# Recurrent layers' block inverse: a level's two products issued one behind the other, the other work in one group after them

## The reference, cut to what matters

```python
def step(state, inp):
    r_t, w_t, k_t, v_t, kk_t, b_t = inp
    sa = jnp.einsum('bhvk,bhk->bhv', state, kk_t)
    state = (state * w_t[:, :, None, :] - sa[..., None] * b_t[:, :, None, :]
             + v_t[..., None] * k_t[:, :, None, :])
    y = jnp.einsum('bhvk,bhk->bhv', state, r_t)
    return state, y
```

## Time and profile before

| | |
|---|---|
| median of 3 runs | 976.15 us (975.79 to 976.30) |
| the profiled execution | 976.48 us |
| its span | 974.7 us |
| PE busy | 963.9 us, 99% |
| DVE busy | 734.9 us, 75% |
| ACT busy | 529.9 us, 54% |
| granted clock of PE | 0.998 of full speed |
| inverse of l = 1, y of level 1 to y of level 5 | 372.72 to 400.73 us |
| inverse of l = 2, the same | 700.10 to 728.11 us |

### The profile page before, as it was taken

The page is one execution under the profiler, slowest core; times in us unless marked ns, Lnnn a source line. Parts: engine busy times, 40 slices in busy tenths (PEclk is TensorE's granted clock), DMA queues, the critical chain, the costliest instruction groups (busy, mean ns, idle before and its releaser), DMA issues.

```text
span 974.7 us, 17484 instructions
## 1 busy us (share of the span) xinstructions
PE 963.9 (99%) x7270; PEld 865.5 (89%) x7270; DVE 734.9 (75%) x1253; ACT 529.9 (54%) x806; POOL 6.8 (1%) x13
## 2 busy tenths in 40 slices
PE   9999999999999999999999999999999999999997
PEld 8999898888888989889988888898887998888886
DVE  6978688877785998867787875568978578787653
ACT  6486566556454653656556553365546466555431
POOL 1000000000000000000000000000000000000000
PEclk9999999999999999999999999999999999999999
DMA  9744445555554332224555455443231255545531
GB/s 339 205 156 170 160 162 198 194 177 206 179 182 158 118 111 88 88 87 144 204 196 205 176 190 200 173 168 115 77 116 54 94 209 187 202 173 197 192 130 44
DMA packets 24823, 156.55 MB, mean 161 GB/s; under 512 B 2736, under 2 KB 4536, under 8 KB 7208
## 3 DMA queue, kind: packets, MB, share of 16 engines
q1 hardware_dynamic: 22320, 151.64, 44.3%
q10 hardware_dynamic: 2072, 2.49, 1.2%
q0 software_dynamic: 352, 1.31, 0.4%
HBM read 153.99 MB, written 1.44 MB: 159 GB/s over the span
## 4 chain that ended last, share of the span: by engine, by line
PE 93%; DVE 3%; issue 1%; ACT 1%; DMA 1%; SPq 0%; DVEq 0%; ACTq 0%
PE bank L507 27%; PE bank L720 22%; PE bank L725 11%; PE bank L751 11%; PE bank L753 6%; PE bank L578 2%; PE bank L1004 1%; PE bank L1022 1%; DVE w_lo L1817 1%; DVE arena L1799 1%; PE bank L583 1%; PE bank L1011 1%; PE bank L965 1%; PE bank L1225 1%; DMA raw<-in_w 1%
## 5 line engine op out<-in xcount | busy, mean ns | idle before, releaser
L1817 DVE TENSOR_TENSOR w_lo<-raw,w_hi 128x2048 fp32r<-128x2048 f32 (+2 forms) x142 | 319.0, 2249 | 111.7 <-ACT w_hi L1288 111.3
L1288 ACT ACTIVATE w_hi<-raw 128x2048 fp32r<-128x2048 f32 (+4 forms) x153 | 273.3, 1788 | 98.6 <-PE bank L753 68.7
L720 PE MATMUL bank<-h_both,w_hi 128*128 128x512 f32 x912 | 228.4, 392 | 0.1
L720 PEld LDWEIGHTS bank<-h_both,w_hi 128*128 128x128 f32 x912 | 164.0, 189 | 29.6 <-issue 0.3
L507 PE MATMUL bank<-h_both,w_hi 128*128 128x256 f32 x880 | 164.0, 287 | 0.2 <-DVE w_lo L1817 0.2
L1288 ACT ACTIVATE arena<-bank 128x256 f32<-128x256 f32 (+3 forms) x189 | 74.0, 403 | 163.6 <-PE bank L725 118.5
L751 PE MATMUL bank<-act_both,w_hi 128*128 128x512 f32 x462 | 162.3, 393 | 0.0
L507 PEld LDWEIGHTS bank<-h_both,w_hi 128*128 128x128 f32 x880 | 137.2, 191 | 5.2 <-issue 2.1
L725 PEld LDWEIGHTS bank<-h_both,w_lo 128*128 128x128 f32 x912 | 124.4, 190 | 8.9
L753 PE MATMUL bank<-act_both,w_lo 128*128 128x256 f32 x462 | 130.6, 283 | 0.0
L725 PE MATMUL bank<-h_both,w_lo 128*128 128x256 f32 x912 | 127.2, 282 | 0.0
(11 more groups left out here) (332 smaller groups left out, 1234.8 us busy)
## 6 DMA issues: line engine op xcount, KB each, us to landing
raw<-in_w SPq DMA_DIRECT2D x136, 1024.0 KB, 4.9
raw<-in_w SPq DMA_DIRECT2D x2, 896.0 KB, 4.5
raw<-in_w SPq DMA_DIRECT2D x3, 512.0 KB, 3.7
raw<-in_w SPq DMA_DIRECT2D x2, 768.0 KB, 4.3
cst<-in_consts SPq DMA_DIRECT2D x1, 1120.0 KB, 11.1
raw<-in_first SPq DMA_DIRECT2D x4, 256.0 KB, 4.7
x<-in_first SPq DMA_DIRECT2D x4, 256.0 KB, 4.9
arena<-bias_rows ACTq DMA_DIRECT2D x4, 256.0 KB, 5.8
```

Of the source, the lines that this page charges most:

```text
L720: pe.matmul(to, hi(k), h_both[:, :, k, :], start=(k == 0), stop=False, skip_group_check=True)
L1288: return act.activation(dst, src, ACT.Copy, **kw)
L1817: dve.tensor_tensor(w_lo[:, s, 0:n], raw[:, s, 0:n], w_hi[:, s, 0:n].bitcast(F32), ALU.subtract)\
```

## The change

On PE, `back_products(n)` follows the y of its level directly for n = 1 to 4, and both halves of `beside_inverse(l, n, ...)` (at n = 1 the whole of `project(l, 8)`) follow behind it. At n = 5 the scores stay between y and `back_products(5)`. y waits for `inv_xt` of the level below; the mark `inv_x` and DVE's wait for it are gone. On DVE the four subtractions of a level move ahead of the level's work beside it, for n = 1 to 4. Two weight splits move too: ACT's `hi_of` of (l, "out", 0) stands ahead of the copies of `up(0)` and `up(1)` instead of behind them; `hi_of` of (l, "out", 1) leaves level 3 for a place behind `exponential(l, 3)`, and DVE's `lo_of` of it goes from ahead of `logits_of(4, 5)` to behind `bonus_and_gain()`.

```diff
-        AFTER_LEVEL = {2: ("out", 0)}
...
                     for q in range(2):
 
                         pe.wait_ge(V.sem, V.at(l, "inv_bt", n, q))
-                        pe.wait_ge(A.sem, A.at(l, "inv0", q)) if n == 1 else pe.wait_ge(V.sem, V.at(l, "inv_x", n - 1, q))
+                        pe.wait_ge(A.sem, A.at(l, "inv0", q)) if n == 1 else pe.wait_ge(V.sem, V.at(l, "inv_xt", n - 1, q))
...
+                    if n == 5:
+                        beside_inverse(l, n, 0)
+                    back_products(n)
                     if n == 1:
-                        project(l, 8, between=lambda: back_products(1))
-                        continue
-                    beside_inverse(l, n, 0)
-                    back_products(n)
-                    if n == 5:
-
-                        break
-                    beside_inverse(l, n, 1)
+                        project(l, 8)
+                    elif n < 5:
+                        beside_inverse(l, n, 0)
+                        beside_inverse(l, n, 1)
...
                             copy(swap_q[:, 0, :], flat(b["qr"])).then_inc(A.sem, A.mark(l, "swap", 2))
-                            hi_of(CHUNK[l, "out", 1])
...
                     for q in range(2):
                         inverse_y(n, q)
+                    if n == 2:
+                        hi_of(CHUNK[l, "out", 0])
                     beside_inverse(n)
-                    if n in AFTER_LEVEL:
-                        hi_of(CHUNK[l, *AFTER_LEVEL[n]])
...
                 exponential(l, 3)
+                hi_of(CHUNK[l, "out", 1])
                 turned(l, 2)
...
-                    beside_inverse(n, 0)
+                    if n == 5:
+                        beside_inverse(n, 0)
                     for q in range(2):
...
-                        after_m(l, "inv_zt", n, q)
+                        else:
+                            after_m(l, "inv_zt", n, q)
                         tt(*(blocks(v, n, 1) for v in (q4(XT, q), q4(XT, q), quads(2 + q)[:, :, 0:64])),
                            ALU.subtract, l, "inv_xt", n, q)
-                        if n == 5:
-                            continue
-                        dve.wait_ge(V.sem, V.at(l, "inv_xt", n, q))
-                        dve.nop().then_inc(V.sem, V.mark(l, "inv_x", n, q))
+                    if n < 5:
+                        beside_inverse(n, 0)
                     beside_inverse(n, 1)
...
                 probs_of(2, 3)
-                lo_of(CHUNK[l, "out", 1])
                 logits_of(4, 5)
...
                 bonus_and_gain()
+                lo_of(CHUNK[l, "out", 1])
```

## The result

| | before | after |
|---|---|---|
| median | 976.54 us (15 runs, 975.79 to 977.21) | 978.28 us (15 runs, 977.95 to 978.68) |
| span of the profiled execution | 974.7 us | 976.6 us |
| PE busy | 963.9 us | 963.5 us |
| y of level 1 to y of level 5, l = 1 | 28.01 us | 27.68 us |
| y of level 1 to `take_off(0)` | 34.94 us | 35.41 us |

The ratio is 1.0019, with an interval of 1.0012 to 1.0026: the changed kernel is slower by 1.74 us. That is just inside the 0.2% that the prediction took as the least that can be told from no change; the interval is narrower than that and excludes no change. All 15 runs of before have a median of 976.54, rather than the 976.15 of the first three.

What follows compares the result with a forecast made beforehand. PE, busy 99% of the span, bounds the kernel. Per layer the inverse gains 0.2 inside a first term of 0.5 to 0.6; the second adds 0.4 to 0.5; 0.95 taken, 1.9 in all, giving 978.1 us, range 975.4 to 980.2.

Steps and rivals of the forecast that it cites:

- the 0.2%: Whole kernel: the least difference, 1.95 us, that a measurement was taken to tell from no change; slower began at 978.1.
- The wait for the copy: PE behind y, levels 1 to 4: pauses 0.22 each for ACT's copy, 0.22 more at level 2; 1.10 per layer.
- The inverse: PE, levels 1 to 4: 1.28 per layer removed less 1.10 of new waiting, a gain of 0.2 us per layer.
- The sum of trips: PE, levels 1 to 4: one small-tile trip spared per level, 0.31 each, 0.22 at level 3; 1.15 per layer.
- The split of (l, "out", 0): DVE behind level 4's subtractions: rotate(3) 0.75 late, take_off(0) 0.6 later, the inverse's gain included; +0.6 per layer.
- The slack: Chain from rotate(3) to take_off(0): 0.11 between the end of negated(0, 0) and take_off(0), with 0.05 for the semaphore.
- The split of (l, "out", 1): DVE behind bonus_and_gain(): idle 0.38 and 0.70, negated(1, 0) 1.08 later, take_off(1) +0.5 per layer; nothing on ACT.
- The sum: Whole kernel: terms of 0.5 to 0.6 and 0.4 to 0.5, taken as 0.95 per layer, 1.9 us slower in all.
- the larger wait: Rival, levels 1 to 4: copy late or PE slower, 0.1 to 0.3 more per level; 980 to 981 us; chance 0.13.
- the first rival: Chain to take_off(0): DVE's delays do not reach PE, only the inverse's 2 x 0.2 gain counts; 975.8 us; chance 0.2.
- DVE's delays do not reach PE: Rival: the chain to take_off(0) has more room than read, only the inverse counts; 975.8 us; chance 0.2.
- the spared trips alone decide: Rival, inverse: copies not waited for, DVE's splits hidden, 2.6 us saved; 973.6 us; chance 0.07.

Runs made afterwards that it cites:

- e6: The changed kernel with 4 idle 64x64 matmuls added between y and the back products at levels 1 to 4: 978.31 us, ratio 1.0018 to the kernel before.
- e7: The changed kernel with 8 idle 64x64 matmuls added between y and the back products at levels 1 to 4: 979.63 us, ratio 1.0032 to the kernel before.
- e10: Changed kernel, both DVE splits moved, level 2's y copied before cq_hi's rounding, first-half copies of y in two 128-column pieces: 974.72 us, 0.9980 to before.
- e3: The changed kernel with both weight splits moved to other places, PE's new order kept: 975.93 us against 976.53 for before, ratio 0.9993.
- e9: The kernel before with only ACT's hi_of of (l, "out", 0) put ahead of the copies of up(0) and up(1): 976.59 us against 976.67, ratio 1.0000.
- e1: The changed kernel with DVE's lo_of of (l, "out", 0) moved from behind level 4's subtractions to ahead of level 3's: 976.74 us, ratio 1.0004 to before.
- e2: Changed kernel, (l, "out", 1) split on DVE back ahead of logits_of(4, 5), on ACT behind level 5's copies of y: 977.61 us, 1.0011 to before.
- e5: The changed kernel with ACT's hi_of of (l, "out", 0) back behind the copies of up(0) and up(1): 985.93 us, ratio 1.0097 to the kernel before.
- e4: The changed kernel with both weight splits moved and PE's order of the kernel before put back: 978.54 us, ratio 1.0022 to the kernel before.

## Why the prediction was right

**The wait for the copy** was priced at 1.16 from y to the back products, 1.38 at level 2, 1.10 a layer. Measured are 1.16 three times and 1.37, and e6, e7 and e10 show the pause from three sides: work put into it costs nothing up to its size, everything beyond it, and a shorter copy gives it back.

**The inverse** gained 0.33 a layer where 0.2 were forecast. Levels 1 and 4 gained 0.12 each, for 0.09 forecast; the terms that were mis-sized are those of levels 2 and 3. At level 2 the forecast was a loss of 0.13 (0.31 for a trip against 0.44 for the wait), and the level gained 0.06. The first two full-array products of `up(0)` stand there. Before, on PE:

```profile
384.07 0.51 PE L507 MATMUL bank<-h_both,w_hi 128*128 128x256 f32 x2
384.42 0.28 PE L507 MATMUL bank<-h_both,w_lo 128*128 128x256 f32 x1
```

and what they read, on DVE, before:

```profile
382.99 1.03 DVE L1799 TENSOR_TENSOR h_both<-spare,h_both 128x512 fp32r<-128x512 f32 x2
```

After, on PE:

```profile
386.34 0.39 PE L504 MATMUL bank<-h_both,w_hi 128*128 128x256 f32 x2
386.57 0.28 PE L504 MATMUL bank<-h_both,w_lo 128*128 128x256 f32 x1
```

0.35 for two products before and 0.23 after, although they follow other full-array products in both. Before, DVE was through with `h_both` at 384.02, and PE began 0.05 later: PE waited here for DVE, in a pause too short for the waits view, and after the change it comes later and doesn't. The product ahead of them also holds PE 0.05 longer before (0.51 against 0.46). Together that is 0.17 of the 0.19 by which level 2 was mis-sized. The sum of trips had no term for that. (That the slow pair comes from the wait is read from these rows; no run tried it.)

At level 3 it was the other way round: 0.13 were forecast as gain (0.22 for the trip, 0.13 for the pause that goes, less 0.22 for the wait), and 0.03 came. The trip was too dear. The new order puts `up(2)` directly in front of `k_rot`, which uses 64x128 tiles:

```profile
393.86 0.28 PE L504 MATMUL bank<-h_both,w_lo 128*128 128x256 f32 x1
394.07 0.70 PE L1181 MATMUL bank<-arena,cst 64*128 64x256 f32 x2
```

0.21 between them, where neighbours of the full array start 0.12 apart: 0.09, the price of getting into smaller tiles once more. In the old order `k_rot` followed the back products, so this change of tile is new, and the trip saves 0.13 rather than 0.22. The other 0.01 is rounding. The mechanism stands, and e3 and e9 size it: of e3's 0.34 the rounding's place is 0.13 and the order of the rest 0.21. That the forecast for the whole inverse missed by no more than 0.13 owes something to luck: one missing term gave 0.19 more, the other took 0.09.

**The split of (l, "out", 0)** was to make `rotate(3)` 0.75 late and `take_off(0)` 0.6. Measured from y of level 1, `rotate(3)` is 0.59 late (29.04 against 28.45) and `take_off(0)` 0.47. The slack was right: 0.12 are lost between the two delays where 0.11 had been read. Too large was the delay at the start, by 0.16: the three levels ahead had won 0.21 instead of 0.15, and the split follows the second half's subtractions 0.40 after their start (399.30 to 399.70), not 0.5. From the end of `negated(0, 0)` to `take_off(0)` it is 0.06, where 0.05 had been taken. The 0.8 of new waiting is 0.79 by e1, but the prediction put all of it at `take_off(0)`: it named ACT's copy of the right side as a link to `negated` and did not see that PE itself waits for that copy at `step(0, 0)`, where 0.26 of it falls. The sum is not changed by that, for `take_off(0)` waits longer for the end of the same chain. e1 shows that both waits go with the split.

**The split of (l, "out", 1)** was to hold `negated(1, 0)` back by 1.08 and `take_off(1)` by 0.45. Measured from `take_off(0)`, they are 0.97 (15.59 against 14.62) and 0.39 later. The two idle stretches in front were priced at 0.38 and 0.70 and are 0.29 and 0.63. e2 shows that this wait goes with this split. On ACT the split costs nothing, as priced: it starts at 411.98, is through in 1.90, and ACT is idle for another 0.56 before `turned(2)`, at 414.44, waiting for PE.

**The sum** was 1.9 us for both layers, and it is 1.72 by the trace and 1.74 by the medians. The first term was given as 0.5 to 0.6 and is 0.47, the second as 0.4 to 0.5 and is 0.39. That the absolute forecast lies so near (978.1 against 978.28) is in part luck: the difference was 0.16 too large, and the median of before, on which it stands, was 0.39 higher than in the first three runs.

**The chances.** Half of the forecast and the larger wait make 0.30 + 0.13 = 0.43 for slower, not 0.45, and the other half and the first rival 0.50, not 0.48. The bound of 0.2% was too wide as well: 0.18% came out clear of no change.

**The rivals.** That DVE's delays do not reach PE falls with the four waits of `take_off`. That the spared trips alone decide falls with the 1.16, although e10 shows how near it was: with the splits in a good place and the copy cut to 1.06, three quarters of the 2.6 us that it promised are there. The larger wait was not in this kernel (1.16 at three levels, 1.37 at level 2), but one instruction's place would have made it: in e5 it costs several times what that rival gave it, by another way, since the copy of y stands there behind a weight split.

## What to carry to other kernels

When products that need one another are put next to each other on PE, the round trip through the copying engine becomes visible (here 1.16 us against 0.94 of work): have nothing ahead of that copy, and copy the first piece separately. Then look for the work on the other engines that the new order pushes back: here two weight splits of 2.2 us that nobody needed soon, in front of a chain without slack, cost more than the new order gave. Such filler is to be moved together with the order, and a new order on one engine alone can be worse than the old order on both or the new one on both (e4 against e9 and e3).

## What was not expected of the hardware

**Behind a pause of 1.68 us PE's clock was halved.** In e5 the granted clock fell after PE had stood still for 1.68 us in the middle of dense work, and stayed at the half level for 8 us and parts of the two stretches beside it, while PE was busy. It fell in both layers of the trace, and all four runs of e5 have a lower mean clock (0.992 or 0.996) than any run of the other kernels (0.998 or 0.999). The pauses of 0.22 to 0.59 us in the inverses of the other kernels moved nothing, nor did two of 0.80 and 0.84 elsewhere in the changed kernel (at 122 and 312 us), behind which the clock is 1.00. The Trainium skill ("TensorE: Matmul & The Clock Gate", section "HAM oscillation — how this bites in real kernels") warns of idle gaps that are longer than this one; by that this pause would have cost its own length alone, and the trace doesn't agree. A section behind it in the Trainium skill, "A second HAM failure mode: psum-queue depth-cycling", tells of very short idle times between groups of matmuls that bring the clock down when they come often; e5 has one long pause a layer, so it doesn't describe this case either.

**DVE and POOL on one SBUF operand pair.** In the changed kernel a DVE operation of 256 columns with both operands in SBUF took 1.05 us while POOL was at work. DVE's row, then POOL's:

```profile
396.09 1.05 DVE L1795 TENSOR_TENSOR spare<-spare 128x256 f32<-128x256 f32 x1
```

```profile
395.58 1.28 POOL L487 TENSOR_TENSOR swap_q<-spare,swap_q 128x512 fp32r<-128x512 f32 x1 [269.00 <-ACT swap_q L1284]
```

In the kernel before the same operation starts at the same 396.09 and takes 0.42:

```profile
396.09 0.42 DVE L1799 TENSOR_TENSOR spare<-spare 128x256 f32<-128x256 f32 x1
```

There POOL's ran at 393.66, beside DVE operations with an operand in PSUM, which took 0.48 and 0.49 as elsewhere. The same pair of 1.05 and 1.28 stands in layer 2; in e3, where they overlap for 0.3 us only, it is 0.60 and POOL's 1.40. The Trainium skill has the rule ("GPSIMD Engine Reference", section 1. Specifications): GpSimd shares its SBUF interfaces with VectorE and contends with DVE instructions that have two SBUF inputs. The trace agrees, with 0.6 us for one operation. PE doesn't see it here: DVE's next step (L2308) starts 1.14 after y instead of 0.80, but the subtractions behind that still wait 0.43 for PE's back products.
